# A two-layer transformer block in fp32 on one core: query tiles of one attention session taken from last to first, its causal mask added on GpSimd, and value products issued ahead of the next transposes

## Chip, core and metric

The kernel runs on 1 core of one Trainium2 chip, as one program. The metric is the device time of that core in microseconds; the time before is 1810.9 us, the median of 3 runs.

## What is computed

A token matrix of 512 x 1024 (fp32) goes through a hybrid layer, a gMLP layer and a "forgetting attention" layer, each with its own feed-forward part. The change touches the softmax attention of three places, which the program calls sessions: relative-bias attention (8 heads, causal by chunks), attention of the middle layer over 256 memory rows (4 heads), and in the last layer memory attention (4 heads) followed by forgetting attention (12 heads):

```python
def forgetting_attention(q, k, v, log_f_cum):
    for i in range(s // Q_BLOCK):                       # Q_BLOCK = 128
        q0, q1 = i * Q_BLOCK, (i + 1) * Q_BLOCK
        logits = jnp.einsum("bqhd,bkhd->bhqk", q[:, q0:q1], k[:, :q1]) * scale
        decay = c[:, :, q0:q1, None] - c[:, :, None, :q1]
        logits = jnp.where(qpos >= kpos, logits + decay, -jnp.inf)
        p = jax.nn.softmax(logits, axis=-1)
        outs.append(jnp.einsum("bhqk,bkhd->bqhd", p, v[:, :q1]))
```

Query tile i sees i + 1 blocks of 128 keys, so tile 3 has rows of 512 scores and tile 0 rows of 128. The part of `decay` that belongs to the query row drops out of the softmax; the kernel adds only the part by key, a row that is the same for every query, and masks the last of the blocks (the diagonal one).

## The kernel before

Every engine has its own instruction list, written by hand, and the engines meet through semaphores only. Large products are split into three fp32r matmuls of 128x512 (high by high, low by high, high by low; lines 809 to 811 and, in smaller portions, 872 to 874). Weights come through SyncE's queue, ScalarE makes the high part, VectorE the low part.

**Sessions.** `session(name)` lists the units of a session: one unit is a pair of heads and one query tile `qi` of 128 rows. "rel" has 4 pairs (16 units), "mem_a" 2 pairs, "b" 8 pairs, of which the first two are memory attention (256 keys, no mask) and six are forgetting attention. Units of a pair come in the order qi = 0, 1, 2, 3. Here the units of session "b" are called b0 to b31: b0 to b7 are memory attention, b8 to b31 causal.

**Steps.** Every engine walks the same steps t. In step t TensorE does the following, in this order:

- `scores`, at even t for units t and t + 1 together (line 947: for each of two heads one matmul with K = 64 and 128 to 512 columns), and behind both of them `mask_scores` (line 956: a bf16 matmul of identity by a triangle of -1e30, accumulated onto the diagonal block, 4 for a pair of units). In "b" only.
- `beside(t)`: a portion of a large product. In "b" this is one quarter of a query tile (6 matmuls of 128x512) at t = 0 to 26 except 6, 14 and 22, nothing at t = 27 to 31, and parts of the output product at t = 32 to 35.
- `turn` for unit t - 3 (line 968): transposes of the probabilities, one per key block and head, into bank 6 (head 0) and bank 7 (head 1). It waits until the saves of the unit before it have emptied these banks.
- `values` for unit t - 4 (line 999), if that unit is the last of its pair: the product of all four query tiles of the pair with the values, 8 matmuls. In the last pair of a session tiles 0 to 2 go one step earlier than tile 3.

In step t VectorE does: a quarter of a weight's low part in some steps (line 2055; in "b" t = 1 to 4, 11 to 14, 19 to 22 and 27 to 30), the reciprocals of unit t - 1 (line 2021), `shift_scores` of unit t (line 2012: adds the bias or decay row to the scores in PSUM, with the row maximum), `normalize` of unit t - 1 (line 2028), at t = 3, 8, 12, 17, 21 and 26 the eviction of a query tile (line 1953), and the save of head 1's transposes of unit t - 3 (line 2036). ScalarE does the exponentials of unit t (line 1537), between its two heads the save of head 0's transposes of unit t - 3 (line 1545), the copy of a pair's output (line 1554, in step t for a last unit t - 5), its high part (1559), and halves of weight splits at t = 9, 10, 17, 18, 25 and 26 (line 1567). A save of a pair's first unit also waits until `values` of the pair before it are through, since both use the same cells.

The decay rows of all 12 heads are one tile `decay` of 128 x 12 x 512, the same on every partition, brought by one DMA from GpSimd's queue (line 729). After that GpSimd has nothing to do until the last layer's output.

Of the kernel before, what the change touches and what calls it, by code (L numbers as in the profile page):

```python
# [19 lines left out]
P = 128  # L20
# [81 lines left out]
def program(nc, a, out):  # L102
    ctx = ExitStack()
    with ctx:
# [160 lines left out]
        def p_of(u, h):  # L265
# [51 lines left out]
        def modv(section, t):  # L317
# [95 lines left out]
        tri_set, bf_loaded, decay_stored, decay_back = (  # L413
            sem("tri_set"), sem("bf_loaded"), sem("decay_stored"), sem("decay_back"))
# [146 lines left out]
        def session(name):  # L561

            units = []
            for p in range({s: m for s, m, _ in SESSIONS}[name]):
# [38 lines left out]
        def _(pool):  # L603
# [105 lines left out]
            def mem_load(l, km, vm):  # L709

                for n, t in enumerate((km, vm)):
# [18 lines left out]
                                                   ap=[[0, P], [SEQ, FOX], [1, SEQ]])).then_inc(decay_back, 16)  # L730

# [56 lines left out]
        def _(pe):  # L788
# [151 lines left out]
            def scores(x):  # L940
# [4 lines left out]
                for h in range(2):  # L945
                    rows = slice(HD * h, HD * h + HD)
                    last = pe.matmul(bank[score_bank(u) + h][:, 0:n], x["q"][rows, P * qi:P * (qi + 1)],  # L947
                                     x["k"][rows, 0:n], start=True, stop=True)
                    if not x["mask"]:
                        last.then_inc(scores_ready, 1)  # L950

            def mask_scores(x):

                u, qi = x["u"], x["qi"]
                for h in range(2):
                    pe.matmul(bank[score_bank(u) + h][:, P * qi:P * (qi + 1)], ident_b[:, :],
                              causal_neg[:, :], start=False, stop=True, skip_group_check=True)\
                        .then_inc(scores_ready, 1)

            def turn(x):  # L960

                u, n = x["u"], x["n"]
                for h in range(2):
# [3 lines left out]
                    for kj in range(n // P):  # L967
                        last = pe.transpose(bank[6 + h][:, P * kj:P * (kj + 1)],  # L968
                                            p_of(u, h)[:, P * kj:P * (kj + 1)], ident[:, :])
# [1822 lines left out]
```

## Time and profile before

| | us |
|---|---|
| median of 3 runs | 1810.9 (1809.72 to 1811.01) |
| the profiled execution | 1809.15 |
| its span | 1807.4 |
| TensorE busy | 1770.7, 98% |
| VectorE busy | 1095.2, 61% |
| ScalarE busy | 732.5, 41% |
| GpSimd busy | 40.6, 2% |
| mean granted clock of TensorE | 0.999 of 2.4 GHz |

The execution that was profiled took 1809.15 us, of which 1807.4 are the span of the records and 1.75 lie around it. Session "rel" stands at 165 to 216 us, "mem_a" at 753 to 794, and "b" at 1292.7 to 1397.4. Rows of a timeline give the start of a group of like instructions, the time that it takes, and in brackets the idle time ahead of it with what ended it; since matmuls overlap, the distance from one start to the next is what a group costs TensorE.

### The profile page before, as it was taken

What the parts mean: (1) busy time and instruction counts of PE and PEld (TensorE: products, weight loads), DVE (VectorE), ACT (ScalarE), POOL (GpSimd) and SP (SyncE); (2) the same over time, 40 slices, a digit from 0 to 9 for tenths busy, and PEclk for the clock granted to TensorE, in tenths of its full rate; (3) what the DMA queues carried; (4) which work ended last, traced back from release to release, by engine and by line L of the source; (5) the groups of instructions that cost most, each with busy time, mean ns of one, the idle gap of its engine ahead of it and who ended that gap; (6) DMA issues with size and microseconds to landing.
All of it is one profiled execution on the core that took longest, in us unless ns stands there. A gap on an engine that the chain in (4) does not pass through costs nothing.

```text
span 1807.4 us, 22457 instructions
## 1 busy us (share of the span) xinstructions
PE 1770.7 (98%) x8312; PEld 1427.6 (79%) x8312; DVE 1095.2 (61%) x1601; ACT 732.5 (41%) x1031; POOL 40.6 (2%) x78
## 2 busy tenths in 40 slices
PE   7999899999999999999999999999999999999998
PEld 6887556788888888878888888889766788888887
DVE  6978675656555335775677674245576567767423
ACT  6313663343334323444344443232365434444322
POOL 4110000000000000000000000000000000000000
PEclk9999999999999999999999999999999999999999
DMA  9793112223322323312322222323401232222231
GB/s 346 270 334 134 48 53 100 75 95 106 101 93 87 98 95 94 117 48 94 114 95 93 93 93 90 103 84 110 164 24 48 70 117 93 93 93 93 94 104 70
DMA packets 149081, 195.29 MB, mean 108 GB/s; under 512 B 3646, under 2 KB 133000, under 8 KB 146332
## 3 DMA queue, kind: packets, MB, share of 16 engines
q1 hardware_dynamic: 141272, 155.28, 26.3%
q0 software_dynamic: 7600, 39.13, 5.9%
q8 instruction: 41, 0.67, 0.2%
q14 instruction: 20, 0.16, 0.0%
q10 hardware_dynamic: 148, 0.05, 0.0%
HBM read 189.15 MB, written 5.29 MB: 108 GB/s over the span
## 4 chain that ended last, share of the span: by engine, by line
PE 90%; DVE 5%; DMA 2%; ACT 2%; issue 1%; POOL 0%; ACTq 0%; DVEq 0%
PE bank L809 21%; PE bank L811 20%; PE bank L810 20%; PE bank L872 3%; PE bank L874 2%; PE bank L873 2%; PE bank L1462 2%; PE bank L1463 2%; PE bank L1461 2%; PE bank L947 2%; PE bank L999 1%; PE bank L968 1%; PE bank L852 1%; PE bank L853 1%; PE bank L854 1%; PE bank L1056 1%
## 5 line engine op out<-in xcount | busy, mean ns | idle before, releaser
L1931 DVE TENSOR_TENSOR w_lo<-w_stage,w_hi 128x2048 fp32r<-128x2048 f32 (+3 forms) x135 | 296.8, 2198 | 440.3 <-ACT w_hi L1489 440.0
L809 PE MATMUL bank<-act_hi,w_hi 128*128 128x512 f32 x1232 | 482.2, 391 | 2.4 <-DVE act_lo L2305 0.7
L811 PE MATMUL bank<-act_hi,w_lo 128*128 128x512 f32 x1232 | 479.7, 389 | 0.0
L810 PE MATMUL bank<-act_lo,w_hi 128*128 128x512 f32 x1232 | 479.7, 389 | 0.0
L1489 ACT ACTIVATE w_hi<-w_stage 128x2048 fp32r<-128x2048 f32 (+3 forms) x137 | 251.7, 1837 | 459.6 <-PE bank L811 334.6
L809 PEld LDWEIGHTS bank<-act_hi,w_hi 128*128 128x128 f32 x1232 | 231.3, 188 | 53.9 <-DVE act_lo L1981 2.3
L810 PEld LDWEIGHTS bank<-act_lo,w_hi 128*128 128x128 f32 x1232 | 231.3, 188 | 48.0 <-issue 0.5
L811 PEld LDWEIGHTS bank<-act_hi,w_lo 128*128 128x128 f32 x1232 | 231.3, 188 | 48.0
L811 PE MATMUL bank<-mid_hi,w_lo 128*128 128x512 f32 x352 | 137.0, 389 | 0.0
L809 PE MATMUL bank<-mid_hi,w_hi 128*128 128x512 f32 x352 | 137.0, 389 | 0.0
L810 PE MATMUL bank<-mid_lo,w_hi 128*128 128x512 f32 x352 | 137.0, 389 | 0.0
L1634 ACT ACTIVATE mid_hi<-tmp 128x512 f32 x66 | 40.7, 633 | 98.5 <-DVE tmp L2141 98.5
L811 PEld LDWEIGHTS bank<-mid_hi,w_lo 128*128 128x128 f32 x352 | 66.1, 188 | 13.7
L809 PEld LDWEIGHTS bank<-mid_hi,w_hi 128*128 128x128 f32 x352 | 66.1, 188 | 13.7
L810 PEld LDWEIGHTS bank<-mid_lo,w_hi 128*128 128x128 f32 x352 | 66.1, 188 | 13.7
L1461 PE MATMUL bank<-w_hi,mid_hi 128*128 128x512 f32 x176 | 68.9, 391 | 0.0
L1463 PE MATMUL bank<-w_lo,mid_hi 128*128 128x512 f32 x176 | 68.6, 390 | 0.0
L1462 PE MATMUL bank<-w_hi,mid_lo 128*128 128x512 f32 x176 | 68.5, 389 | 0.0
L1626 ACT ACTIVATE tmp<-tmp,vec 128x512 f32<-128x512 f32 x44 | 33.5, 809 | 70.0 <-DVE tmp L1953 70.0
L1626 ACT ACTIVATE mid_val<-tmp,vec 128x512 f32 x44 | 33.5, 808 | 69.8 <-DVE tmp L1953 69.8
L1953 DVE SCALAR_TENSOR_TENSOR tmp<-bank,rms 128x512 f32<-128x512 f32 x88 | 56.4, 682 | 0.0
L2145 DVE TENSOR_TENSOR mid_lo<-tmp,mid_hi 128x512 f32 x66 | 42.7, 689 | 9.3 <-ACT mid_hi L1634 9.3
(412 smaller groups left out, 2598.5 us busy)
## 6 DMA issues: line engine op xcount, KB each, us to landing
ada_stage<-in_w_ada POOLq DMA_DIRECT2D x24, 1024.0 KB, 6.9
w_stage<-in_w_up SPq DMA_DIRECT2D x22, 1024.0 KB, 5.1
w_stage<-in_a_ffn_in SPq DMA_DIRECT2D x22, 1024.0 KB, 5.1
w_stage<-in_b_ffn_in SPq DMA_DIRECT2D x22, 1024.0 KB, 5.0
w_stage<-in_w_in SPq DMA_DIRECT2D x10, 1024.0 KB, 6.9
w_stage<-in_b_ffn_out SPq DMA_DIRECT2D x10, 1024.0 KB, 5.1
w_stage<-in_w_down SPq DMA_DIRECT2D x8, 1024.0 KB, 5.0
w_stage<-in_a_ffn_out SPq DMA_DIRECT2D x8, 1024.0 KB, 5.0
```

What stands on the lines that cost most here:

```text
L809: pe.matmul(dst, wh, mh, start=start and k == 0, stop=False)
L810: pe.matmul(dst, wh, ml, start=False, stop=False)
L811: last = pe.matmul(dst, wl, mh, start=False, stop=stop and k == nk - 1)
L872: pe.matmul(dst, wh, mh, start=start and k == ks[0], stop=False)
L1461: pe.matmul(dst, mh, hi[:, k, :], start=j == 0 and k == 0, stop=False)
L1462: pe.matmul(dst, ml, hi[:, k, :], start=False, stop=False)
L1463: last = pe.matmul(dst, mh, lo[:, k, :], start=False, stop=j == 5 and k == nk - 1)
L1489: act.activation(w_hi[slot][:, 0:n], raw[:, 0:n], ACT.Copy).then_inc(w_hi_done, 1)
L1626: act.activation(conv_tile(f, i, s, m), conv_src(f, s, m)[:, :], ACT.Identity, scale=w2, bias=b).then_inc(tap_started, 1)
L1931: dve.tensor_tensor(w_lo[slot][:, 0:n], raw[:, 0:n], w_hi[slot][:, 0:n].bitcast(FP32), ALU.subtract).then_inc(w_ready, 1)
L1953: return dve.scalar_tensor_tensor(out=dst, in0=src[:, :], scalar=scale, in1=norm[:, :], op0=ALU.mult, op1=ALU.mult)
L2145: dve.tensor_tensor(mid_lo[:, bass.ds(2 * i + m, 1), :], tmp[:, m, :], mid_hi[:, bass.ds(2 * i + m, 1), :].bitcast(FP32), ALU.subtract).th ...
```

## The change

1. In session "b" the units of a pair come in the order qi = 3, 2, 1, 0, the two memory pairs included. `p_of` goes by `qi` in place of `u % 4`, and what was tied to `qi == 0` or to the last tile is tied to `first` and `last`. The last pair's values are issued as tiles 1 to 3 behind the third unit and tile 0 behind the fourth.
2. The mask matmuls are gone. GpSimd adds the triangle to the diagonal block of the decay row, in place, one 128x128 instruction for each causal unit and head (48 in all). A block must stay unmasked while higher tiles read it, so the instruction for unit u waits until `shift_scores` of unit u - 1 has read (the first of a pair doesn't wait for that). VectorE's `shift_scores` waits for the mask. The wait of VectorE for the decay DMA at t = 8 moves to GpSimd.
3. In all three sessions `values(z)` stands ahead of `turn(y)` in a step.

```diff
@@ p_of
-            if u % 4 == 3:
+            if qi == 3:
                 return (p_high_b if u >= UNIT0["b"] else p_high_0)[:, h, :]
-            if u % 4 == 0 and u >= UNIT0["b"]:
+            if qi == 0 and u >= UNIT0["b"]:
                 return p_mem_b[:, h, :]
-            return cells_of(u, h)[:, P * (7, 10, 13)[u % 4]:]
+            return cells_of(u, h)[:, P * (7, 10, 13)[qi]:]
@@ session
-                for qi in range(NT):
-                    units.append(dict(d, pair=PAIR0[name] + p, u=UNIT0[name] + 4 * p + qi, qi=qi,
+                for n in range(NT):
+                    qi = NT - 1 - n if name == "b" else n
+                    units.append(dict(d, pair=PAIR0[name] + p, u=UNIT0[name] + 4 * p + n, qi=qi,
...
-                                      mask=causal and name == "b", last=qi == NT - 1,
+                                      masked=4 * (p - 2) + n if causal and name == "b" else None,
+                                      first=n == 0, last=n == NT - 1,
@@ gpsimd
+            pool.wait_ge(decay_back, 16)
+            for x in session("b"):
+                if x["masked"] is None:
+                    continue
+                block = slice(P * x["qi"], P * (x["qi"] + 1))
+                for h in range(2):
+                    if not x["first"]:
+                        pool.wait_ge(scores_read, 2 * (x["u"] - 1) + h + 1)
+                    row = decay[:, 2 * (x["masked"] // 4) + h, block]
+                    pool.tensor_tensor(row, row, causal_neg[:, :], ALU.add).then_inc(decay_masked, 1)
@@ tensor
-            def mask_scores(x):
-
-                u, qi = x["u"], x["qi"]
-                for h in range(2):
-                    pe.matmul(bank[score_bank(u) + h][:, P * qi:P * (qi + 1)], ident_b[:, :],
-                              causal_neg[:, :], start=False, stop=True, skip_group_check=True)\
-                        .then_inc(scores_ready, 1)
...
+                if x["u"] >= UNIT0["b"]:
+                    return [0] if x["last"] else [1, 2, 3] if x["qi"] == 1 else []
                 return [3] if x["last"] else [0, 1, 2] if x["qi"] == 2 else []
...
-                for kj in range(x["n"] // P):
+                for kj in range(tiles[-1] + 1 if x["causal"] else NMEM // P):
...
                         for w in together:
                             scores(w)
-                        for w in together:
-                            if w["mask"]:
-                                mask_scores(w)
                     elif fill:
                         fill.pop(0)()
                     if beside:
                         beside(t)
+                    if z:
+                        values(z)
                     if y:
                         turn(y)
-                    if z:
-                        values(z)
@@ vector, shift_scores
+                if x["masked"] is not None:
+                    dve.wait_ge(decay_masked, 2 * x["masked"] + h + 1)
@@ vector, b_beside
-                if t == 8:
-                    dve.wait_ge(decay_back, 16)
```

What moves, as the instruction lists show it. TensorE at the end of "rel", before (`p_high` holds the probabilities of the session's last unit, `cells` the saved transposes; the first rows are the values of tiles 0 to 2):

```order
L968 MATMUL bank<-ident,cells_55 128x128 x3
L968 MATMUL bank<-ident,cells_56 128x128 x3
L968 MATMUL bank<-ident,p_high_147 128x128 x8
L999 MATMUL bank<-cells_55,va_tok 64x384
L999 MATMUL bank<-cells_56,va_tok 64x384
```

and with the change:

```order
L1006 MATMUL bank<-cells_56,va_tok 64x256
L1006 MATMUL bank<-cells_55,va_tok 64x128
L1006 MATMUL bank<-cells_56,va_tok 64x128
L972 MATMUL bank<-ident,p_high_147 128x128 x8
L1006 MATMUL bank<-cells_55,va_tok 64x128
L1006 MATMUL bank<-cells_56,va_tok 64x128
```

The transposes of the last unit have moved behind the six matmuls of tiles 0 to 2, and stand right ahead of the eight of tile 3 that need their saves. TensorE in "b" from step 22 on, before (`qa`, `w` are a quarter of a query tile):

```order
L947 MATMUL bank<-k_b,q_b 128x512 x2
L956 MATMUL bank<-causal_neg,ident_b 128x128 x4
L968 MATMUL bank<-ident,p_high_b 128x128 x8
L872 MATMUL bank<-qa_hi,w_hi_64 128x512
L873 MATMUL bank<-qa_lo,w_hi_64 128x512
```

and with the change:

```order
L961 MATMUL bank<-k_b,q_b 128x256 x2
L961 MATMUL bank<-k_b,q_b 128x128 x2
L972 MATMUL bank<-ident,p_mem_b 128x128 x2
L886 MATMUL bank<-qa_hi,w_hi_64 128x512
L887 MATMUL bank<-qa_lo,w_hi_64 128x512
```

The scores of this step have shrunk from 384 and 512 columns to 256 and 128, the masks are gone, and the unit that is transposed has 2 blocks where it had 8.

## Rows read from the trace of the kernel before

**Rows 1.** Stretches: length, then busy us of PE, PEld, DVE, ACT, POOL; clock; DMA.

```profile
1340.00:1350.00 10.00, 10.00 (x60) 6.80 (x60) 7.15 (x24) 6.65 (x17) 0.00 (x0) 1.00 0.00 0
1370.00:1380.00 10.00, 7.15 (x51) 4.39 (x49) 8.18 (x27) 6.99 (x18) 0.00 (x0) 1.00 0.00 0
```

**Rows 2.** TensorE's timeline, session b, steps 20 to 22: start, us, what.

```profile
1350.63 0.93 PE L947 MATMUL bank<-k_b,q_b 64*128 64x128 f32 x8
1351.49 0.40 PE L956 MATMUL bank<-causal_neg,ident_b 128*128 128x128 bf16 x4
1351.70 0.48 PE L872 MATMUL bank<-qa_hi,w_hi 128*128 128x512 f32 x1
...
1353.17 0.60 PE L968 MATMUL bank<-ident,cells_b 128*128 128x128 f32 x4
...
1355.76 1.77 PE L947 MATMUL bank<-k_b,q_b 64*128 64x384 f32 x8
...
1357.69 1.04 PE L968 MATMUL bank<-ident,p_high_b 128*128 128x128 f32 x8
```

**Rows 3.** VectorE's timeline, session b, step 21.

```profile
1355.89 0.69 DVE L1953 SCALAR_TENSOR_TENSOR q_b<-bank,rms 128x512 f32<-128x512 f32 x1
1356.49 0.55 DVE L2036 COPY cells_b<-bank 128x384 f32<-128x384 f32 x1
```

**Rows 4.** VectorE's groups by shape, 1310 to 1390 us: count, busy, mean ns.

```profile
L2012 DVE CUSTOM_DVE_ANT_0 cells_b<-bank,decay 128x384 f32<-128x384 f32 x12 | 6.2, 553 | 3.6 <-PE bank L956 3.6
...
L2012 DVE CUSTOM_DVE_ANT_0 cells_b<-bank,decay 128x256 f32<-128x256 f32 x12 | 4.6, 418 | 0.0
...
L2028 DVE TENSOR_SCALAR p_high_b<-p_high_b,stats 128x512 f32<-128x512 f32 x12 | 5.3, 482 | 0.0
...
L2028 DVE TENSOR_SCALAR p_mem_b<-p_mem_b,stats 128x128 f32<-128x128 f32 x12 | 2.9, 282 | 0.0
```

**Rows 5.** ScalarE's groups by shape, same stretch.

```profile
L1537 ACT ACTIVATE p_high_b<-p_high_b,stats 128x512 f32<-128x512 f32 x12 | 8.6, 717 | 7.5 <-DVE stats L2012 7.5
...
L1537 ACT ACTIVATE p_mem_b<-p_mem_b,stats 128x128 f32<-128x128 f32 x12 | 4.8, 397 | 0.5 <-DVE stats L2012 0.4
```

**Rows 6.** TensorE's timeline, session b, steps 27, 28, 31 and behind it.

```profile
1373.52 0.44 PE L968 MATMUL bank<-ident,p_mem_b 128*128 128x128 f32 x2 [1.41 <-ACT cells_b L1545]
...
1376.20 0.49 PE L947 MATMUL bank<-k_b,q_b 64*128 64x128 f32 x4
...
1385.36 2.37 PE L999 MATMUL bank<-cells_b,vtok_b 128*64 128x512 f32 x16
...
1397.34 0.50 PE L872 MATMUL bank<-o_hi_b,w_hi 128*128 128x512 f32 x1
```

**Rows 7.** TensorE's timeline, end of session rel.

```profile
212.92 1.13 PE L968 MATMUL bank<-ident,p_high 128*128 128x128 f32 x8 [0.18 <-ACT cells L1545]
213.97 2.39 PE L999 MATMUL bank<-cells,va_tok 128*64 128x384 f32 x28
216.29 3.72 PE L1132 MATMUL bank<-w_mem,mem_again 128*128 128x256 f32 x16
```

**Rows 8.** VectorE's timeline, end of session rel.

```profile
212.77 0.56 DVE L2036 COPY cells<-bank 128x384 f32<-128x384 f32 x1 [0.64 <-PE bank L968]
214.08 0.69 DVE L2036 COPY cells<-bank 128x512 f32<-128x512 f32 x1 [0.75 <-PE bank L968]
```

**Rows 9.** GpSimd's timeline, start of the program.

```profile
14.90 1.31 POOL L648 TENSOR_SCALAR_AFFINE_SELECT tri<-tri 128x128 f32<-128x128 f32 x1
...
17.68 0.29 POOL L648 TENSOR_SCALAR_AFFINE_SELECT ident_b<-ident_b 128x128 bf16<-128x128 bf16 x1
```

**Rows 10.** VectorE's timeline, same stretch.

```profile
12.30 1.23 DVE L2235 CUSTOM_DVE_ANT_0 x_res<-x_tok 128x1024 f32<-128x1024 f32 x1 [2.73 <-DMA x_tok<-in_x]
...
14.84 1.23 DVE L2235 CUSTOM_DVE_ANT_0 x_res<-x_tok 128x1024 f32<-128x1024 f32 x1
```

**Rows 11.** DMA issues, 1270 to 1320 us: KB, us to landing.

```profile
decay<-decay_scratch POOLq DMA_DIRECT2D x1, 3072.0 KB, 12.1
```

More of the change, by code:

```diff
@@ L412, in program @@
             sem("f_plus"), sem("f_summed"), sem("f_saved"))
-        tri_set, bf_loaded, decay_stored, decay_back = (
-            sem("tri_set"), sem("bf_loaded"), sem("decay_stored"), sem("decay_back"))
+        tri_set, bf_loaded, decay_stored, decay_back, decay_masked = (
+            sem("tri_set"), sem("bf_loaded"), sem("decay_stored"), sem("decay_back"), sem("decay_masked"))
         y_tile, y_added, y_gained, gain_loaded = (
@@ L946, in scores @@
                     rows = slice(HD * h, HD * h + HD)
[L947 to L950, printed above, removed]
-            def mask_scores(x):
-                u, qi = x["u"], x["qi"]
-                for h in range(2):
-                    pe.matmul(bank[score_bank(u) + h][:, P * qi:P * (qi + 1)], ident_b[:, :],
-                              causal_neg[:, :], start=False, stop=True, skip_group_check=True)\
-                        .then_inc(scores_ready, 1)
+                    pe.matmul(bank[score_bank(u) + h][:, 0:n], x["q"][rows, P * qi:P * (qi + 1)],
+                              x["k"][rows, 0:n], start=True, stop=True).then_inc(scores_ready, 1)
             def turn(x):
@@ L968, in turn @@
                         last = pe.transpose(bank[6 + h][:, P * kj:P * (kj + 1)],
-                                            p_of(u, h)[:, P * kj:P * (kj + 1)], ident[:, :])
+                                            p_of(x, h)[:, P * kj:P * (kj + 1)], ident[:, :])
                     last.then_inc(pT_ready[h], 1)
@@ L986, in values @@
                 qi = tiles[0]
-                if qi == 0 and (pair > PAIR0["b"] or 0 < pair < PAIR0["mem_a"]):
+                opens = 3 in tiles if pair >= PAIR0["b"] else qi == 0
+                if opens and (pair > PAIR0["b"] or 0 < pair < PAIR0["mem_a"]):
                     pe.wait_ge(out_saved, pair)
-                elif qi == 0 and pair == PAIR0["b"]:
+                elif opens and pair == PAIR0["b"]:
                     pe.wait_ge(group_free, G0["b_q"] + 1)
-                elif qi == 0 and pair == PAIR0["mem_a"]:
+                elif opens and pair == PAIR0["mem_a"]:
                     pe.wait_ge(group_free, G0["a_q"] + 1)
-                elif qi == 0 and pair == PAIR0["mem_a"] + 1:
+                elif opens and pair == PAIR0["mem_a"] + 1:
                     pe.wait_ge(scores_read, 2 * UNIT0["b"] - 2)
                 end = P * (tiles[-1] + 1)
-                for kj in range(x["n"] // P):
+                for kj in range(tiles[-1] + 1 if x["causal"] else NMEM // P):
                     q0 = P * (max(qi, kj) if x["causal"] else qi)
@@ L1010, in softmax @@
                     x, y, z = (unit_at(units, t - lag) for lag in (0, TURN_LAG, VALUE_LAG))
-                    if x and name == "b" and x["qi"] == 0 and t >= 8:
+                    if x and name == "b" and x["first"] and t >= 8:
                         pe.wait_ge(q_saved, t // 4 - 1)
@@ L1535, in exps @@
                 c = (2 * u + h) % 8
-                p = p_of(u, h)[:, 0:n]
+                p = p_of(x, h)[:, 0:n]
                 act.activation(p, p, ACT.Exp, scale=-1.0, bias=neg_max[:, c:c + 1],
@@ L1542, in save_pT @@
                 act.wait_ge(pT_ready[0], u + 1)
-                if x["qi"] == 0 and x["pair"]:
+                if x["first"] and x["pair"]:
                     act.wait_ge(out_ready, x["pair"])
@@ L2010, in shift_scores @@
                     dve.wait_ge(pT_ready[h], u - RING + 1)
+                if x["masked"] is not None:
+                    dve.wait_ge(decay_masked, 2 * x["masked"] + h + 1)
                 c = (2 * u + h) % 8
-                dve.tensor_tensor_reduce(out=p_of(u, h)[:, 0:n], in0=bank[score_bank(u) + h][:, 0:n],
+                dve.tensor_tensor_reduce(out=p_of(x, h)[:, 0:n], in0=bank[score_bank(u) + h][:, 0:n],
                                          in1=x["bias"](x["qi"], h), scale=-1.0, scalar=3.0e38, op0=ALU.add,
@@ L2026, in normalize @@
                 for h in range(2):
-                    p = p_of(u, h)[:, 0:n]
+                    p = p_of(x, h)[:, 0:n]
                     dve.tensor_scalar(p, p, row_inv[:, (2 * u + h) % 8:(2 * u + h) % 8 + 1], None,
@@ L2033, in save_pT @@
                 dve.wait_ge(pT_ready[1], u + 1)
-                if x["qi"] == 0 and x["pair"]:
+                if x["first"] and x["pair"]:
                     dve.wait_ge(out_ready, x["pair"])
```

3 lines of the change are left out of this document (2 added, 1 removed).

## The prediction, as it was put on record

> **What bounds the kernel now.** First the busy times by stretch. Over most of session "b" TensorE has no gap: from 1340 to 1350 us it is busy for 10.00 of 10 us at a granted clock of 1.00, beside 7.15 of VectorE and 6.65 of ScalarE; from 1370 to 1380, where no more query quarters fill its steps, it has 7.15 and VectorE 8.18 [rows 1]. Then the timelines, for the order in which the three engines hand a unit on. TensorE's shows what a group costs it: scores of 128 and 256 columns 0.86 us (1350.63 to 1351.49), the four masks behind them 0.21, scores of 384 and 512 columns 1.93 less 0.21, so 1.72 [rows 2]. Eight transposes last 1.04 us and four 0.60, so one costs 0.11 [rows 2]. VectorE's and ScalarE's timelines show how near the hand-over is to being late: in step 21 VectorE starts its save of unit b18 at 1356.49, is done some 0.5 us later, and TensorE wants it at 1357.69 for the transposes of b19 [rows 2, 3]. That leaves 0.7 us, and on this the prediction turns. What counts as a difference is 0.2% of the time, about 3.6 us.
>
> **The change, part by part.** The sum is made against the profiled execution, 1809.15 us; the median of the runs shown stands 1.75 above it.
>
> *Masks.* 48 matmuls go, 12 groups of 0.21 us: at most 2.5 us. In steps 8 to 22, where TensorE is full, 8 groups are worth 1.7 us. Two more (steps 24 and 26) give 0.4. The last two stand in a stretch that VectorE paces and are covered there.
>
> *Order of the tiles, steps 8 to 23.* A pair's columns are the same in sum, but who waits for whom isn't. At an even step that opens a pair the scores now have 512 and 384 columns. Taken from rows, VectorE's save of unit b18 comes later, counted from the start of step 20, by:
> - the scores 0.86 longer, less the masks 0.21: 0.65;
> - one more transpose for head 0 of b17: 0.11;
> - an exponential of 512 columns in place of 128 that stands between that save and VectorE's next step, 717 against 397 ns: 0.32 [rows 5], and ScalarE's save of 3 blocks in place of 2, 0.1 (the slope of the same rows);
> - two shifts of 384 in place of 256 columns, 553 against 418 ns: 0.27; two normalizations of 512 in place of 128, 482 against 282 ns: 0.40 [rows 4]; its own save of 2 blocks in place of 3: -0.13.
>
> That is 1.7 us later, while TensorE arrives 0.4 us sooner (two mask groups). The spare 0.7 becomes a wait of 1.4 us at step 22, which has no quarter to hide it. Step 14 is alike but without the eviction of 0.69 us [rows 3] in VectorE's step before, and TensorE itself comes later there, since quarter 13 has to wait for an eviction: 0.5. At steps 10 and 18 a quarter of 1.47 us (1351.70 to 1353.17) stands ahead of the transposes and hides all of it [rows 2]. Behind the two waits VectorE still has a weight part, shifts, normalizations and a save to do, some 2.2 us, before the pair's values can start, and TensorE only 1.8 us (2 transposes and a quarter): 0.4 more, twice. Two items are small: at step 13 the wait for the evicted tile hides 0.2 us behind two more transposes, and at step 23 the unit that opens the pair has 8 transposes where it had 2, of which 6 x 0.11 = 0.65 us are paid before step 24 instead of later. Sum to step 24: -1.7 + 1.4 + 0.5 + 0.8 - 0.2 + 0.65 = +1.45 us.
>
> *Steps 24 to 27.* The wait of 1.41 us at step 27 [rows 6] looks like the place for a gain, since the unit saved there shrinks from 512 to 128 columns. It isn't: ScalarE stands in its weight half, released by the last quarter, and the save comes behind that half and one exponential. The wait stays, some 0.2 us longer because ScalarE's exponential and VectorE's save are both asked for by the values. With two mask groups off: -0.2.
>
> *Steps 28 to 31.* VectorE paces these. From the scores at 1376.20 to the pair's values at 1385.36 are 9.16 us [rows 6]. At the start VectorE now has behind it a 128-column shift and a 256-column normalization, 1.4 us that it still had ahead of it before; in exchange shifts of 512, 384, 256 for 128, 256, 384 columns are 0.8 more and normalizations 0.15 more: -0.45.
>
> *The tail.* Behind those values come 8 transposes (0.85 us) that were 2 and stood ahead of them; then 12 transposes where there were 18: -0.65. The last values shrink and the output parts cover the short saves. From 1385.36 to the first matmul of the second output chunk at 1397.34 TensorE is full now [rows 6]: +0.2. Session b in all: 1.45 - 0.2 - 0.45 + 0.2 = +1.0.
>
> *Values ahead of transposes.* Inside a session nothing comes of it: both wait for the same saves, so the pair of groups starts and ends where it did. At a session's end it matters. In "rel" the transposes of the last unit run at 212.92 and hide under them the end of VectorE's save of 212.77; then 28 instructions of values run back to back, 213.97 to 216.29 [rows 7, 8]. With the change the first 12 of them (1536 of 2560 columns, 1.4 us) wait for that save, about 213.3; transposes 214.7 to 215.75; VectorE's save, which now starts 0.11 behind the transposes' end and takes 0.69 [rows 8], ends at 216.55 with nothing beside it on TensorE; tile 3 takes 0.9: 217.4 in place of 216.29. That is +1.1, and the memory product behind it, 16 instructions of 3.72 us, moves with it [rows 7]. In "mem_a" a quarter stands between the last transposes and the last values: 0. In "b" the last unit now has 2 transposes: 0.
>
> *GpSimd.* Its trace has no addition of two tensors. The nearest rows are its selects over the same 128x128: 0.29 us, and 1.31 us for one that ran while VectorE multiplied two SBUF tensors [rows 9]. VectorE's instruction of that kind lasted 1.23 us both before that and beside it, so VectorE lost nothing [rows 10]. The mask for head h can start when the shift of the unit before has read, and VectorE has 2.0 us or more of other work until it needs it, so 0.3 to 0.6 us is hidden. I take 0; below nothing is excluded, since the mask is added work. At 1.31 each, the two of a unit need 2.6 us against 2.0 to 2.2: up to 0.6 a unit. The decay rows land 12.1 us after their issue at about 1282.5 [rows 11], 18 us before the first causal unit.
> The Trainium skill ("SBUF — State Buffer", section "SBUF: two separate sides") says that GpSimd and a VectorE instruction with two SBUF inputs or in its two-port mode exclude each other for a whole instruction, the loser blocking fully. The select of 1.31 us agrees for GpSimd as the loser; no row here shows VectorE losing. By the Trainium skill's "GPSIMD Engine Reference", section "Elementwise — side-by-side cycle accounting", a two-input addition takes about 2.6 cycles an element, from which I estimate 0.3 us for the body here; the sum would be the same.
>
> *Sum.* +1.1 + 1.0 + 0 = +2.1: 1811.25 for an execution like the profiled one, 1813.0 beside the median.
>
> **The rivals.**
> *VectorE is not late (a gain).* If it keeps its 0.7 us of room at steps 14 and 22 (my 1.7 us would have to be under 0.7), the 2.7 us there go, and shorter tail units take up to 1.5 of the 2.9 us that TensorE is idle from 1370 to 1380 [rows 1]. Session b then gives -1.7 to -3.2 us, the whole -0.6 to -2.1: 1809 to 1810. With "rel" untouched too, which would take an end with slack behind it, 1807.7. For it: that idle time is there. Against it: every term of the delay has its row. Chance 0.22; of that over 0.2% only 0.09.
> *GpSimd sets VectorE's pace (slower).* Place: VectorE's shift of each causal unit. Each mask costs 1.3 us, because VectorE's normalizations and splits, both SBUF to SBUF, keep it out. It decides from about 1.0 us a mask on, where two exceed the 2.0 us. Then a unit is 0.4 to 0.6 late in the some 9 places that VectorE already times (each pair's second unit, steps 28 to 31): +3.6 to +5.4 on top of 2.1: 1816.6 to 1818.4. For it: one row of 1.31. Against it: reads from PSUM leave GpSimd gaps. Chance 0.13.
> *GpSimd holds VectorE up.* A mask that gets in between two of VectorE's SBUF instructions delays the second by its own length, 0.3 us: in the same 9 places +2.7, so 1815.7. (The Trainium skill's page "SBUF — State Buffer", cited above, has this rule.) For it: the second head's mask falls just where normalizations start. Against it: rows 10. Chance 0.1.
>
> **The numbers.** My forecast, 1811 to 1815 us, has 0.55; the gain 0.22, the two GpSimd cases 0.13 and 0.1. 1813.0 is the predicted time. The range 1807.5 to 1817 takes in the first rival whole and the second's near half. Faster by over 0.2% (under 1807.3) 0.10; within 0.2% 0.72; slower (over 1814.5) 0.18, the GpSimd cases less those with only part of the price.
>
> **What would show it.** Right: TensorE idle at step 22 ahead of transposes of 2 blocks, released by VectorE's save, 1 us or more; the same about 0.5 us at step 14; about 0.9 us of idle between the last transposes and the last values of "rel"; the wait of 1.4 us at step 27 still there, now ahead of values; masks of 0.3 to 0.6 us on GpSimd and no shift waiting for one. Wrong: no idle at step 22, a stretch from the scores of step 20 to the second output chunk shorter than its 46.7 us of before (1350.63 to 1397.34), shifts released by GpSimd, or normalizations above 482 ns at 512 columns.

## The result and the profile after

The changed kernel takes 1818.5 us (median of 5, 1817.67 to 1820.13) where the kernel before takes 1810.9 beside it: the ratio is 1.0047, with a 95% interval of 1.0036 to 1.0058. It is slower by 7.6 us, and the forecast of 1813.0 with its range to 1817 was too low.

The profiled execution takes 1818.54 us, 9.4 more than the one of before. 0.85 of it stands ahead of any changed code (the first scores of "rel" start at 166.32 for 165.47, one execution's drift), 1.64 in "rel", 0 in "mem_a", and 6.9 in session "b". Below, **S** is the stretch from the scores of step 8 to the first matmul behind the session's last values; it was 85.9 us (1311.45 to 1397.34) and is 92.7 (1314.02 to 1406.68).

TensorE's timeline of the changed kernel in session "b" (start, length, the group, and in brackets the idle time ahead with what ended it):

```profile
1348.63 0.47 PE L886 MATMUL bank<-qa_hi,w_hi 128*128 128x512 f32 x1 [1.16 <-DVE q_b L1957]
...
1363.31 0.33 PE L972 MATMUL bank<-ident,p_mem_b 128*128 128x128 f32 x1 [1.04 <-DVE cells_b L2042]
...
1365.78 2.38 PE L1006 MATMUL bank<-cells_b,vtok_b 128*64 128x512 f32 x16 [0.74 <-ACT cells_b L1549]
...
1379.25 2.37 PE L1006 MATMUL bank<-cells_b,vtok_b 128*64 128x512 f32 x16 [1.64 <-ACT cells_b L1549]
...
1391.76 3.92 PE L1006 MATMUL bank<-cells_b,vtok_b 128*64 128x512 f32 x16 [2.00 <-ACT cells_b L1549]
1395.61 1.09 PE L972 MATMUL bank<-ident,p_high_b 128*128 128x128 f32 x8
...
1405.41 0.50 PE L886 MATMUL bank<-o_hi_b,w_hi 128*128 128x512 f32 x1 [0.98 <-DVE o_lo_tok L2054]
```

The wait at step 22 (1.04 us, at 1363.31) is there as foreseen. Three lines were not: a quarter at step 18 that waits 1.16 us for VectorE's eviction, values at step 31 that take 3.92 us where the same 16 matmuls take 2.37 at step 27, and an output part at 1405.41 that waits for a low part.

Where values wait, at 1365.78 and 1391.76, the rows name ScalarE. Values need the saves of both engines, though, and VectorE's came last. At 1391.76 ScalarE's save had ended at 1391.04, and VectorE's is

```profile
1391.38 0.28 DVE L2042 COPY cells_b<-bank 128x128 f32<-128x128 f32 x1
```

so it ended at 1391.66. At 1365.78 it is alike: ScalarE's save had ended at 1365.05, VectorE's at 1365.68.

The 3.92 us of values at step 31 are a matter of the clock. Busy times of 4 us each, the changed kernel:

```profile
core 0: us, PE busy (x) PEld busy (x) DVE busy (x) ACT busy (x) POOL busy (x), PEclk, DMA share, GB/s
1384.00:1388.00 4.00, 2.69 (x20) 1.36 (x16) 4.00 (x15) 2.41 (x6) 1.27 (x3) 1.00 0.00 0
1388.00:1392.00 4.00, 1.84 (x8) 1.06 (x10) 4.00 (x13) 2.83 (x11) 1.53 (x3) 0.51 0.22 54
1392.00:1396.00 4.00, 4.00 (x20) 1.77 (x19) 1.26 (x8) 0.49 (x2) 0.00 (x0) 0.64 0.60 208
```

TensorE is busy for 2.69 and 1.84 of 4 us, the granted clock is at its lower level (0.50, 1.2 GHz) from about 1388 to 1395, and the values of that time take 1.55 us more than at 2.4 GHz, from their start to that of the transposes behind them. The kernel before has 1.00 throughout, with more work in the same place:

```profile
1384.00:1388.00 4.00, 3.23 (x20) 1.64 (x21) 3.74 (x12) 2.23 (x8) 0.00 (x0) 1.00 0.78 262
```

(The Trainium skill, "TensorE: Matmul & The Clock Gate", section "What's actually happening", says that the clock is gated by how busy the engine has been; this trace agrees: the fall to 0.50 follows 2.69 busy us of 4.)

The end of "rel", for [rows 7]:

```profile
214.34 1.52 PE L1006 MATMUL bank<-cells,va_tok 128*64 128x384 f32 x12 [0.70 <-ACT cells L1549]
215.79 1.09 PE L972 MATMUL bank<-ident,p_high 128*128 128x128 f32 x8
217.75 1.09 PE L1006 MATMUL bank<-cells,va_tok 128*64 128x128 f32 x16 [0.88 <-DVE cells L2042]
218.78 3.50 PE L1136 MATMUL bank<-w_mem,mem_again 128*128 128x256 f32 x15
```

VectorE and GpSimd by shape in 1300 to 1400 us (count, busy us, mean ns), for [rows 4]:

```profile
L744 POOL TENSOR_TENSOR decay<-decay,causal_neg 128x128 f32<-128x128 f32 x46 | 22.3, 498 | 72.5 <-DVE stats L2018 72.2
...
L2018 DVE CUSTOM_DVE_ANT_0 p_high_b<-bank,decay 128x512 f32<-128x512 f32 x12 | 7.7, 683 | 0.8 <-PE bank L961 0.8
L2034 DVE TENSOR_SCALAR p_high_b<-p_high_b,stats 128x512 f32<-128x512 f32 x12 | 6.3, 566 | 0.0
...
L2034 DVE TENSOR_SCALAR cells_b<-cells_b,stats 128x384 f32<-128x384 f32 x12 | 5.8, 520 | 0.0
...
L2034 DVE TENSOR_SCALAR p_mem_b<-p_mem_b,stats 128x128 f32<-128x128 f32 x12 | 3.9, 363 | 0.0
```

No shift waits for a mask, but normalizations of 512 columns now take 566 ns for 482 and those of 128 columns 363 for 282 [rows 4]; those of 384 take 520 where the kernel before has 415. Those of 256 columns are as before (346 ns for 348), and so are VectorE's weight parts (682 for 685). The timelines of GpSimd and VectorE show why the 256 columns are spared: four additions run in a row, and the normalizations of 256 columns start just behind them:

```profile
1364.33 2.27 POOL L744 TENSOR_TENSOR decay<-decay,causal_neg 128x128 f32<-128x128 f32 x4 [2.29 <-DVE stats L2018]
1366.72 0.61 DVE L2034 TENSOR_SCALAR cells_b<-cells_b,stats 128x256 f32<-128x256 f32 x2
```

### The profile page after: what moved, and what is told of

Read it like the earlier page. It is cut to its first block, busy times and chain, and to the rows that moved or that the text cites. A ratio compares the mean times of both kernels' runs of the same rounds, so it can differ in the third digit from the quotient of the medians.

```text
span 1816.8 us, 22392 instructions
## 1 busy us (share of the span) xinstructions
PE 1773.1 (98%) x8256; PEld 1427.7 (79%) x8256; DVE 1098.4 (60%) x1601; ACT 732.1 (40%) x1031; POOL 63.7 (4%) x126
## 4 chain that ended last, share of the span: by engine, by line
PE 92%; DVE 5%; ACT 1%; issue 1%; DMA 0%; SPq 0%; ACTq 0%; DVEq 0%
PE bank L823 21%; PE bank L824 21%; PE bank L825 21%; PE bank L886 2%; PE bank L1467 2%; PE bank L1465 2%; PE bank L1466 2%; PE bank L888 2%; PE bank L887 2%; PE bank L1006 2%; PE bank L961 1%; PE bank L866 1%; PE bank L867 1%; PE bank L868 1%; PE bank L972 1%
```

## The experiments

Each kernel was timed in 5 rounds. In the table, "vs before" is its median less that of the kernel before in the same group of runs; S comes from its profile; "lower clock" is how much longer its values of step 31 take than at 2.4 GHz (2.3 us, start to start), and its eight transposes too where they stand ahead of the values (1.0 us). S and the lower clock are those of one profiled execution each, the first column is a median.

| kernel | vs before, us | S, us | lower clock, us |
|---|---|---|---|
| changed | +7.6 | 92.7 | 1.55 |
| e1 transposes first | +5.5 | 90.6 | 2.4 |
| e2 part 3 alone | +3.8 | 87.9 | 0 |
| e3 masks on TensorE | +9.2 | 93.0 | 1.4 |
| e4 order alone | +4.8 | 91.9 | 3.0 |
| e5 filler | +6.9 | 91.1 | 0 |
| e6 no masks | +8.1 | 91.8 | 2.2 |
| e7 additions twice | +9.9 | 93.3 | 1.6 |
| e10 values first inside | +0.3 | 86.3 | 0 |
| e11 low parts later | +9.4 | 92.6 | 1.7 |
| e13 eviction first | +9.1 | 92.2 | 1.8 |
| e15 transposes first, filler | +3.1 | 89.5 | 1.2, see below |

**The three parts apart.** The theory was: part 3 costs at the end of "rel", the order makes VectorE late, GpSimd slows normalizations. e1 is

```diff
-                    if z:
-                        values(z)
                     if y:
                         turn(y)
+                    if z:
+                        values(z)
```

on the changed kernel, e2 the reverse on the kernel before; e3 is the changed kernel with `mask_scores` back on TensorE and no addition on GpSimd, and e4 has both, so only the order.

> The changed kernel with the transposes ahead of the values again in all three sessions (part 3 undone). Theory (part 3 costs only at the end of the relative-bias session, where the last values and the first save no longer cover each other; the trace shows 1.6 us there): 1816.5 to 1817.2, with the memory product starting about 216.8 us and session b as long as in the changed kernel. Rival (the order of values and transposes also costs in session b, where values now hold the transposes of the next pair's first unit up behind two saves): session b shrinks by 2 us or more and the time is under 1815.

Measured 1815.6 (ratio 1.0033, 1.0021 to 1.0045), between the two. S is 2.0 us shorter, as the rival had it, and 2.9 with each one's lower clock taken off.

> The kernel before with part 3 alone. Theory: the end of the relative-bias session costs 1.6 us and nothing else moves: 1812.0 to 1813.0. Rival (the cost depends on session b too): 1814 or more. Rival (the 1.6 us are drift of one execution): 1811.

Measured 1813.9 (1.0023, 1.0014 to 1.0032): more than the theory. "rel" is 1.64 us longer, and S 2.0, which the forecast had at nothing. TensorE's timeline of e2:

```profile
1388.31 2.38 PE L999 MATMUL bank<-cells_b,vtok_b 128*64 128x512 f32 x16 [1.31 <-ACT cells_b L1545]
...
1397.70 1.09 PE L968 MATMUL bank<-ident,p_high_b 128*128 128x128 f32 x8
1400.18 0.50 PE L872 MATMUL bank<-o_hi_b,w_hi 128*128 128x512 f32 x1 [1.38 <-DVE o_lo_tok L2048]
```

and VectorE's behind those transposes:

```profile
1398.83 0.69 DVE L2036 COPY cells_b<-bank 128x512 f32<-128x512 f32 x1 [3.30 <-PE bank L968]
1399.44 0.68 DVE L2048 TENSOR_TENSOR o_lo_tok<-sq_sum,o_hi_b 128x512 fp32r<-128x512 f32 x1
```

The output part at 1400.18 needs the low part of the pair before, and VectorE makes that only behind its save of the session's last transposes. In the kernel before 1.5 us of values lie between these transposes and the part, and no wait stands ahead of the part.

> The changed kernel with the masks back on TensorE as 48 small matmuls; descending order and part 3 stay, GpSimd idle. Theory (GpSimd's masks stretch VectorE's normalizations by 0.2 us a unit, and in the steps that VectorE paces this is paid): normalizations of 512 columns are back at 0.88 us a pair, VectorE's shares give back 3 to 4 us, TensorE pays 1.7 to 2.5 for the masks: 1815.5 to 1817.5. Rival (GpSimd costs nothing, all the loss is the order): 1820 to 1821, since the masks come on top.

> The descending order alone: masks on TensorE, transposes ahead of values. Theory (the order makes VectorE's hand-over late at the second unit of each pair, some 3 us in all, beside GpSimd's share and the 1.6 us of part 3): 1813.5 to 1815.5. Rival (the order by itself is nearly free and GpSimd carries the loss in session b): 1811 to 1812.

Measured 1819.3 and 1814.9. e4 came out as expected, but its profile shows that 3.0 of its 6.0 us more in S are the lower clock. e3 lies between its theory and its rival. Its normalizations of 512 columns are back at 480 ns, as the theory had it, and yet it gains nothing: beside the kernel before it is 1.6 us over the changed kernel, within the intervals of both, and in S, less the lower clock, 0.5 us (91.6 and 91.1). GpSimd's masks are nearly as dear as TensorE's.

**Part 3 inside and at the ends.** e10 is e2 with the old order for the last pair of each session:

```diff
-                    if z:
+                    if z and not z["final"]:
                         values(z)
                     if y:
                         turn(y)
+                    if z and z["final"]:
+                        values(z)
```

> The kernel before with the values ahead of the transposes in all pairs but the last of each session. Theory (that order costs only where a session ends, since there the last save and the product behind it have no cover: 1.6 us in the relative-bias session, 1.4 to 1.6 in the last one; inside a session 0.1 us a pair): 1810.3 to 1811.3. Rival (it costs in every pair, because values wait for VectorE's save and the first transposes wait for ScalarE's only): 1812.5 or more.

Measured 1810.8 (1.0007, 0.9998 to 1.0016), as the theory: in the kernel before, the order of values and transposes inside a session costs 0.4 us in S. All of it is there by step 24 (51.58 us from the scores of step 8, for 51.14). The wait ahead of step 31's values, 1.31 us in e10 as in e2 above where 0.88 stood ahead of the transposes, adds nothing, since two transposes (0.65 us) have moved behind it. Values need both engines' saves; the first transposes need ScalarE's only and cover the rest of VectorE's. (Its "rel" took 51.44 us for 50.82, but so did that of e1, 51.38, which has the order of before there: a difference between executions.)

This does not carry over to the descending order. There part 3 costs 1.3 us by step 24 (55.09 us for e1's 53.82): the two waits of 0.75 and 0.74 us ahead of a pair's values, at steps 15 and 23, are in the changed kernel and not in e1, where the eight transposes stand ahead of the values and cover them.

**The clock.** e5 adds matmuls in which nothing is computed that is used:

```diff
+                if t in (29, 31):
+                    pe.wait_ge(q_saved, 6)
+                    for _ in range(3 if t == 29 else 6):
+                        pe.matmul(bank[1][:, :], qa_hi[:, 0, 0:P], qa_hi[:, 1, :], start=True, stop=True)
```

> The changed kernel with matmuls that compute nothing needed (128x512, into a bank that is free there and is overwritten later): 3 at step 29 and 6 at step 31, ahead of the transposes and the values that wait there. Theory (in all four kernels with the descending order the granted clock falls to 0.50 for 4 to 6 us after the idle of steps 27 to 31, and this costs 1.6 us in the changed kernel and 2.4 to 3 us where transposes go first): TensorE stays busy, the clock stays at 1.00, the values of step 31 take 2.4 us and not 3.9, and though 2.1 us of work are added the time is 1816.5 to 1817.5. Rival (the lower clock has another cause than the idle): it is as low as before and the time 1818.5 to 1820.

Measured 1817.1, as the theory. Beside the kernel before that is 0.7 us less than the changed kernel, which the intervals (1.0024 to 1.0052 and 1.0036 to 1.0058) do not separate; the traces do. The busy times of e5 and its timeline:

```profile
1384.00:1388.00 4.00, 3.91 (x22) 2.17 (x21) 3.91 (x11) 3.02 (x9) 0.86 (x2) 1.00 0.00 0
1388.00:1392.00 4.00, 2.98 (x17) 1.86 (x16) 4.00 (x16) 2.42 (x7) 1.31 (x3) 1.00 0.00 0
```

```profile
1390.78 1.64 PE L1436 MATMUL bank<-qa_hi 128*128 128x512 f32 x6
1393.17 2.38 PE L1006 MATMUL bank<-cells_b,vtok_b 128*64 128x512 f32 x16 [0.74 <-ACT cells_b L1553]
1395.47 1.09 PE L972 MATMUL bank<-ident,p_high_b 128*128 128x128 f32 x8
```

The fillers lie in the idle time and the clock stays at 1.00. The values of step 31 start at the same point as in the changed kernel, 77.75 us behind the scores of step 8 for 77.74, and take 2.38 us for 3.92. S is 91.1: the changed kernel's 92.7 less its 1.55. So the size of the lower clock's price is shown, and that here the fall goes when the idle time is filled.

> Descending order and GpSimd's masks, transposes first, with the filler matmuls of the run 'filler'. It leaves of the change only the order and the masks, without the lower clock and without part 3. Theory (the order makes VectorE and ScalarE late at steps 9 to 31 by 3 to 4 us, the mask matmuls give back 1.5 to 2, GpSimd takes 1 of it again): clock 1.00, transposes of step 31 1.1 us and values 2.4, the time 1812.3 to 1813.7, 1.8 to 3.2 over the kernel before. Rival (the rest of the loss is the clock's too): 1810.0 to 1811.5.

Measured 1813.4 (1.0017, 1.0008 to 1.0026), in the theory's range, though the clock was not held: with the same nine fillers it fell at about 1385.4, and six of them took 2.91 us at the lower level. They outlasted the wait: the transposes behind them start 76.9 us from the scores of step 8 for e1's 75.9, and take 0.2 us more than at 2.4 GHz; the values, at 2.4 GHz again, take 2.38. So 1.2 us of its S are the fillers' doing, and the order and the masks alone are +2.3 us in S (89.5 less 1.2, and e1's 90.6 less 2.4, against 85.9). The median, +3.1, still has the fillers' share in it. Fillers that hold the clock in one kernel need not hold it in another.

**GpSimd.** e6 is the changed kernel without the additions on GpSimd: no causal mask is applied in session "b". e7 adds, ahead of each mask, `pool.tensor_tensor(neg_upper[:, :], ident[:, :], causal_neg[:, :], ALU.add)` into a tile no longer read.

> The changed kernel without any causal mask in the last attention session: no addition on GpSimd, no mask matmul, and VectorE waits for the decay rows once. Theory (GpSimd's additions stretch the normalizations that they meet by 0.2 us a unit, and those steps in which TensorE waits for VectorE or ScalarE pay for it): pairs of 512-column normalizations take 0.88 us in place of 1.05 and the time is 1816.3 to 1817.3. With the masks on TensorE (1819.3) this makes the mask matmuls worth 2 to 3 us. Rival (GpSimd costs nothing): 1818.0 to 1819.0.

> The changed kernel with twice as many additions on GpSimd: ahead of each mask one more 128x128 addition into a tile that is no longer needed. Theory (VectorE loses about 0.1 us for each addition that runs beside its normalizations and splits): pairs of 512-column normalizations take 1.1 to 1.3 us and the time is 1820 to 1822; the masks then end so late that some shifts wait for them. Rival (VectorE's longer normalizations are hidden): 1818.0 to 1819.0 with shifts still waiting for nothing.

Measured 1818.2, the rival's number, and 1820.1, the theory's. By shape, e6 and then e7:

```profile
L2005 DVE CUSTOM_DVE_ANT_0 p_high_b<-bank,decay 128x512 f32<-128x512 f32 x12 | 7.8, 684 | 0.7 <-PE bank L950 0.6
...
L2021 DVE TENSOR_SCALAR p_high_b<-p_high_b,stats 128x512 f32<-128x512 f32 x12 | 5.3, 482 | 0.0
```

```profile
L2039 DVE TENSOR_SCALAR p_high_b<-p_high_b,stats 128x512 f32<-128x512 f32 x12 | 6.3, 566 | 0.0
...
L2039 DVE TENSOR_SCALAR p_mem_b<-p_mem_b,stats 128x128 f32<-128x128 f32 x12 | 4.7, 430 | 0.0
```

Without GpSimd the normalizations are back at 482 ns, while the shifts, which read PSUM, take 683 to 684 with it and without. Doubling it leaves 512 columns at 566 and lengthens 128 columns from 363 to 430 and 256 columns from 346 to 390: it matters whether a normalization meets an addition, more than how many there are. e13 below shows the same from the other side: at step 18 the eviction stands ahead of the normalizations, the additions (1346.28 to 1347.18) are through when these start (1347.19), and two of 512 columns take 0.87 us together and not 1.05.

In S, less each one's lower clock, the masks on GpSimd cost 91.1 - 89.6 = 1.5 us and the mask matmuls 91.6 - 89.6 = 2.0. The 1.5 us can be placed: 1.0 by step 24 (55.09 for 54.10), where the clock is 1.00 in both, and 0.55 from the scores of step 28 to the values of step 31 (9.18 for 8.63). In the medians this cannot be seen (+7.6 and +8.1 beside the kernel before). The profiled execution of e6 has the deeper fall of the clock, 2.2 for 1.55 us; whether the others have it too is not known. In e7 shifts of 128 columns wait 0.6 us in all for GpSimd, but its pairs of 512 columns aren't slower than the changed kernel's, where the theory had 1.1 to 1.3 us. (The Trainium skill, "SBUF — State Buffer", section "SBUF: two separate sides", lets GpSimd and a VectorE instruction in a two-port mode or with two SBUF inputs exclude each other, so that whichever comes second waits until the other's instruction is through. Here the mean loss was 81 to 105 ns for a normalization of 512, 384 or 128 columns, under the 0.43 us of an addition that runs alone. That VectorE loses time to GpSimd is now shown; whether each loss is the rest of an addition is not.)

**What makes VectorE late.** e11 puts `split_quarter` of the first output chunk at steps 23 to 26 (`(C0["b_out"], 19)` becomes 23); e13 puts `evict(t)` ahead of `normalize(w)` in "b".

> The changed kernel with VectorE's four low parts of the first output chunk at steps 23 to 26 in place of 19 to 22. Theory (in steps 18 to 22 VectorE is behind because these 0.68 us instructions stand ahead of its shifts; the waits of TensorE at steps 18 and 22, 1.2 and 1.04 us, are theirs): the wait at step 22 falls under 0.4 us and the time is 1817.0 to 1817.8. Rival (the chain of scores, exponentials and normalization sets step 22, or steps 23 to 26 lose what 19 to 22 gain): 1818.3 or more.

> The changed kernel with the eviction of a query tile ahead of VectorE's normalizations, in the last session only. Theory (with the descending order the eviction stands behind 1.05 us of 512-column normalizations while the next quarter waits for it, 0.44, 0.22 and 1.16 us at steps 9, 13 and 18): these three waits nearly go, the wait at step 22 stays since its save stands behind both, and the time is 1816.6 to 1817.6. Rival (the normalizations, 0.68 us later, delay the transposes and give it back): 1818.2 or more.

Measured 1820.0 and 1819.3, both the rival's number. e11's waits at steps 18 and 22 are 1.16 and 1.04 us, unchanged to the last digit. VectorE, relieved of its low part, waits there itself (e11, VectorE):

```profile
1360.55 0.17 DVE L2027 RECIPROCAL stats<-stats 128x2 f32<-128x2 f32 x1 [0.34 <-ACT p_high_b L1541]
...
1361.66 1.05 DVE L2034 TENSOR_SCALAR p_high_b<-p_high_b,stats 128x512 f32<-128x512 f32 x2
1362.63 0.68 DVE L1957 SCALAR_TENSOR_TENSOR q_b<-bank,rms 128x512 f32<-128x512 f32 x1
1363.23 0.41 DVE L2042 COPY cells_b<-bank 128x256 f32<-128x256 f32 x1
```

For these two waits it is a chain, not a load: scores of 512 columns, two shifts, two exponentials, the reciprocals, two normalizations, the eviction, and only then the save that TensorE wants. The low parts do have a share elsewhere, and the rival's second half names it: with them moved, the wait of 0.74 us ahead of step 23's values falls to 0.16 (step 24 comes 0.7 us sooner), and the wait at step 27 grows from 1.64 to 2.04, so that 0.2 us are left by step 28.

In e13 only one of the three waits goes: that of step 18 falls from 1.16 to 0.20 us, those of steps 9 and 13 stay at 0.44 and 0.22, and that of step 22, which was to stay, is 0.87. By step 28 the kernel is 0.7 us ahead of the changed one, and 0.5 in S, with a lower clock 0.3 us deeper. Part of this is the normalizations that no addition meets any more, so e13 doesn't price the eviction alone. The median shows no gain.

**Filling the idle time with real work.** e8, on the kernel before, issues output parts early and parts of the second chunk in their stead:

```diff
-            B_OUT_KS = [[6, 7], [0, 1], [2, 3], [4]]
+            B_OUT_KS = {27: [6], 29: [7], 31: [0], 32: [1, 2], 33: [3], 35: [4]}
+            B_OUT_KS2 = {33: [6], 34: [7, 0]}
```

e12 also moves three of VectorE's low parts of that chunk to steps 31 to 33 (and its three second-chunk parts to step 34). e9 is e1 with e8's edit, e14 e1 with e12's.

> The kernel before with real work in the idle time of steps 27 to 31: the output product's parts for k = 6, 7 and 0 move from steps 32 and 33 to 27, 29 and 31, and parts of its second chunk take their places. Theory (TensorE idles 1.4 us at step 27, 1.4 in steps 28 and 29 and 0.9 at step 31 for saves that come when they come): 2.1 us of work fit in there and the time is 1807.8 to 1808.8. Rival (the tail then waits for the saves of the last pair, which set its end): 1810 or more.

> The kernel before with the output parts early, and besides three of VectorE's four low parts of the second output chunk moved from steps 28 to 30 to steps 31 to 33. Theory (VectorE paces steps 28 to 31, and each of these instructions is 0.68 us of that pace, while VectorE idles in the tail): 1.0 to 2.0 us under the run 'parts early', 1806.5 to 1807.5. Rival (steps 28 to 31 go by the chain of saves, not by VectorE's load): 1808.3 to 1808.8.

> The changed kernel with the transposes first (as in the run 'turn first') and with output parts moved to steps 27, 29 and 31 as was done to the kernel before. Theory (the lower clock of this end cost 2.4 us, and the idle of steps 27 to 31 takes 2.1 us of real work): the clock stays at 1.00 through step 31 and the time is 1810.7 to 1811.7, 4 to 5 us under the same kernel without the move, where the kernel before gained 1.7. Rival (the idle moves into the tail with the parts): 1813.5 or more.

> Descending order and GpSimd's masks, transposes first, with both moves of the run 'vector moved': output parts early, and three of VectorE's low parts at steps 31 to 33. Theory (the order's own price is 2 to 3 us in steps 8 to 26 and stays; the idle of steps 28 to 31 and with it the lower clock go): 1808.8 to 1810.3, clock 1.00 throughout the session, and still over the kernel before with the same two moves (1807.5). Rival (the shorter tail units pay once VectorE is relieved): under 1807.3.

| kernel | median, us | ratio to before | lower clock, us |
|---|---|---|---|
| e8 | 1808.5 | 0.9991 (0.9982 to 1.0000) | 0 |
| e12 | 1807.5 | 0.9985 (0.9976 to 0.9994) | 0 |
| e9 | 1811.6 | 1.0006 (0.9997 to 1.0015) | 1.6 |
| e14 | 1811.3 | 1.0006 (0.9997 to 1.0015) | 0 |

e12 beats both kernels, by 3.0 us the one before and by some 11 the changed one. e8 came as expected, at the edge of what its interval can tell from no gain, and e12 at the edge of its range. e9's time is as expected, its clock isn't: the part at step 27 waited 1.3 us for the evicted bank and filled nothing, and the clock fell at step 31 all the same. e14 has that wait too, held the clock at 1.00 and still takes 3.8 us more than e12 (1 more than expected). In S it is 2.8 us (88.4 for 85.6), and 2.7 of them are there by step 24 (53.82 for 51.11), ahead of both moves: the descending order is the slower one also without the lower clock and without part 3.

## Why the prediction was wrong

Three steps failed, each a cost that I took as nothing: part 3 in "b" (put at 0, measured 2.9 us), GpSimd's additions (put at 0, 1.5 us) and the tail's clock, which had no term (1.55 us). They overlap in part, since GpSimd's price was measured with part 3 in place.

In S, with the lower clock taken off, the order alone is +3.0 (e4), the masks' move -0.7 (e1 against e4) and part 3 +2.9 (the changed kernel against e1). Together these are 5.2, and 1.55 of lower clock make the 6.8 by which S grew. They add up by construction, each being the difference of two kernels. "rel" has 1.64 and the drift 0.85.

Up to step 24 the clock is 1.00 everywhere and executions repeat to 0.01 us (e1, e9, e14 and e15 have 53.81 or 53.82, the changed kernel and e5 55.09 and 55.10), so this stretch separates the parts best:

| kernel | from the scores of step 8 to those of step 24, us |
|---|---|
| before | 51.14 |
| e2 part 3 alone | 51.56 |
| e4 order alone | 53.93 |
| e1 order, masks on GpSimd | 53.82 |
| e6 order, part 3, no masks | 54.10 |
| changed | 55.09 |
| e3 order, part 3, masks on TensorE | 55.17 |

- *"Order of the tiles, steps 8 to 23", with the masks: +1.45 to step 24.* It measured 3.95 on the changed kernel and 2.7 without part 3 (e1). The mechanism is right where it was looked for: VectorE's save is late, and the wait at step 22 was 1.04 us for 1.4, at step 14 0.17 for 0.5, the two waits ahead of a pair's values 0.75 and 0.74 for 0.4 each. What it had wrong is step 18. "At steps 10 and 18 a quarter ... stands ahead of the transposes and hides all of it", but the quarter of step 18 itself waits 1.16 us for the eviction of step 17, which now stands behind 1.05 us of normalizations. GpSimd has 1.0 us of the 3.95 (the changed kernel against e6), most of it inside these waits: in e6 those ahead of values are 0.53 us, that of step 18 is 0.96 and that of step 22 0.87. With the waits as measured in place of those forecast the sum comes to 2.5; the other 1.4 us are not itemised. A part of them is that a group costs more or less by what follows it: in the changed kernel four transposes ahead of a quarter take 0.35 us (1322.57 to 1322.92) and ahead of scores 0.52 (1360.37 to 1360.89).
- *"Steps 24 to 27": -0.2.* Right: from the scores of step 24 to those of 28, 13.47 us for 13.61.
- *"Steps 28 to 31": -0.45.* 9.18 us for 9.16, so 0; GpSimd's additions beside the normalizations account for it, since without them (e6) it is 8.63.
- *"The tail … TensorE is full now: +0.2."* 14.9 us for 12.0. 1.55 are the lower clock, which I did not look for, though I counted the idle time that brings it; 0.98 are the wait for the low part of the pair before.
- *"Values ahead of transposes": "rel" +1.1, in "b" 0.* "rel" was 1.64, of which 1.5 lie at its end, with the wait ahead of the last values where I put it (0.88 us); my steps there were short by up to 0.2 us each, the last one's 16 instructions with 1.03 us for 0.9. In "b" it was 2.0 on the kernel before and 2.9 on the changed one. "Inside a session nothing comes of it: both wait for the same saves" is false: the first transposes of a unit need ScalarE's save only, the values need VectorE's too, and that costs 0.4 us by step 24 on the kernel before and 1.3 on the changed one. My own sum had "0.4 more, twice" ahead of a pair's values, but I booked it with the order of the tiles; e1 shows that it is there only with part 3. At the end of "b" I looked only at how many transposes the last unit has, not at what VectorE has queued behind their save.
- *"GpSimd: I take 0"*, since "VectorE lost nothing" in [rows 10]. The sign that I named for being wrong, normalizations above 482 ns, came: VectorE lost 81 to 105 ns for each of 512, 384 and 128 columns. The masks lasted 0.5 us, no shift waited, and the price, 1.5 us in S, was hidden in instructions that wait for nobody. Of the rivals "GpSimd holds VectorE up" (2.7 us) comes nearest, with a smaller loss at more places. "GpSimd sets VectorE's pace" has a time, 1816.6 to 1818.4, that the measured 1818.5 all but meets, and that is chance: its masks of 1.3 us and its waiting shifts did not come.
- *"VectorE is not late (a gain)"* is out: the waits of 1.16 and 1.04 us for it are there, and e14 shows no gain even with real work in the tail's idle time.

What stays open: the lower clock's depth differs between kernels (1.4 to 3.0 us in those of the table that have it), each known from one execution only, so medians of kernels that have it compare only to about a microsecond; why nine fillers held the clock in e5 and not in e15; and how much of e14's 3.8 us is GpSimd, which was not tried apart.

## What to carry to other kernels

Where engines hand work on through a chain, an edit that leaves TensorE waiting can cost twice, as here: it waits, and then it comes out of the wait at half its clock. Real work moved into the idle time is the thing to try: e12, with three of VectorE's low parts moved as well, gained 3.0 us on the kernel before. Before two pieces of work change places, ask at each end of the loop what covers the last save, and what the saving engine has queued behind it. Work given to GpSimd was paid for by those of VectorE's SBUF-to-SBUF normalizations that it ran beside, so read their mean by shape and not only the waits. And where an engine's wait names one releaser, look at when the other's work ended too.

## What the hardware showed that I had not expected

The granted clock fell to 0.50 at about 1388 us without any long gap: in the 4 us ahead TensorE had been busy for 2.69, its longest wait since the values of step 27 was 0.77 us, and in steps 23 to 27 it was 1.64. It did so in every kernel with the descending order but e5 and e14 (in e15 while the fillers ran). In the kernel before it stayed at 1.00 with 2.9 us of idle in ten [rows 1]. And GpSimd's additions lengthened the normalizations of VectorE that they met by 17 to 29% (512 and 128 columns), the doubled ones hardly those of 512 and 384 further (566 and 529 ns) but those of 256 and 128, while VectorE's shifts, which read PSUM, did not feel them (683 ns with them, 684 without).
